# One 128x128 stationary shape for all attention products: zero-padded keys, values in pairs of heads, the forgetting decay in the padded rows

## The reference

```python
# forgetting attention: a decay is added to the logits of each head
log_f = log_sigmoid(f_logit + b_f)
cum = cumsum(log_f, axis=1)                       # (B, H_FOX, S)
logits = einsum('bhqd,bhkd->bhqk', q, k) * scale + cum[..., :, None] - cum[..., None, :]
out = einsum('bhqk,bhkd->bhqd', masked_softmax(logits, causal), v)

# dilated windows, differential attention, selected keys: the same two products
qk = rms_norm(q, gain_q), rms_norm(k, gain_k)
logits = einsum('bqhe,bkhe->bhqk', *qk) * 64 ** -0.5 + bias     # masked with -inf
out = einsum('bhqk,bkhe->bqhe', softmax(logits), v)
```

## Time and profile before

| | |
|---|---|
| median of three runs | 2591.96 us (2590.84 to 2592.58) |
| span of the profiled execution | 2591.7 us |
| TensorE busy in it | 2371.6 us |
| VectorE busy | 1063.7 us |
| ScalarE busy | 963.4 us |
| GpSimd busy | 388.2 us |
| TensorE's mean granted clock | 0.955 |

### The profile page before, as it was taken

One profiled execution on the slowest core, in us unless ns is written; L12 is line 12 of the kernel. 1 busy time (PEld: TensorE's weight loads), 2 busy tenths in 40 slices (PEclk: granted clock), 3 DMA queues, 4 the chain that ended last, 5 costly groups with the idle time before them and its releaser, 6 DMA issues. The chain is left out here.

```text
span 2591.7 us, 30357 instructions
## 1 busy us (share of the span) xinstructions
PE 2371.6 (92%) x11019; PEld 1828.8 (71%) x11019; DVE 1063.7 (41%) x1957; ACT 963.4 (37%) x1410; POOL 388.2 (15%) x375
## 2 busy tenths in 40 slices
PE   6699887999799989899999999984899998999999
PEld 3479684567388868578878787951557886788787
DVE  6484444343554432332223333148464334333322
ACT  2133213343455532344432212348456433444311
POOL 0010321131122210111110000124241000122200
PEclk7798998999899999899999999997999999999999
DMA  6871001101133333123333233200011323233331
GB/s 231 287 211 41 1 1 46 57 1 33 57 90 96 97 94 100 33 81 97 97 93 101 75 88 97 82 13 17 13 54 52 95 80 98 82 96 97 94 101 64
DMA packets 348925, 210.42 MB, mean 81 GB/s; under 512 B 21293, under 2 KB 329699, under 8 KB 348798
## 3 DMA queue, kind: packets, MB, share of 16 engines
q1 hardware_dynamic: 347691, 208.37, 27.0%
q10 hardware_dynamic: 1139, 0.82, 0.1%
HBM read 206.48 MB, written 9.24 MB: 83 GB/s over the span
## 5 line engine op out<-in xcount | busy, mean ns | idle before, releaser
L236 PE MATMUL ffn_up_psum<-h_hi,ffn_up_w_hi 128*128 128x512 f32 x704 | 275.3, 391 | 0.0
L237 PE MATMUL ffn_up_psum<-h_lo,ffn_up_w_hi 128*128 128x512 f32 x704 | 274.1, 389 | 0.0
L238 PE MATMUL ffn_up_psum<-h_hi,ffn_up_w_lo 128*128 128x512 f32 x704 | 274.1, 389 | 0.0
L331 DVE TENSOR_TENSOR ffn_up_w_lo<-ffn_up_raw,ffn_up_w_hi 128x1024 fp32r<-128x1024 f32 x88 | 107.7, 1225 | 326.5 <-ACT ffn_up_w_hi L327 326.5
L327 ACT ACTIVATE ffn_up_w_hi<-ffn_up_raw 128x1024 fp32r<-128x1024 f32 x88 | 93.1, 1060 | 165.6 <-PE ffn_up_psum L238 162.4
L236 PEld LDWEIGHTS ffn_up_psum<-h_hi,ffn_up_w_hi 128*128 128x128 f32 x704 | 132.6, 188 | 28.8 <-DVE ffn_up_w_lo L331 1.3
L237 PEld LDWEIGHTS ffn_up_psum<-h_lo,ffn_up_w_hi 128*128 128x128 f32 x704 | 132.3, 188 | 28.2 <-issue 0.6
L238 PEld LDWEIGHTS ffn_up_psum<-h_hi,ffn_up_w_lo 128*128 128x128 f32 x704 | 132.3, 188 | 27.1
L236 PE MATMUL ffn_down_psum<-ffn_hidden_hi,ffn_down_w_hi 128*128 128x512 f32 x352 | 138.2, 392 | 0.0
L236 PE MATMUL conv_up_psum<-h_hi,conv_up_w_hi 128*128 128x512 f32 x352 | 137.6, 391 | 0.0
L237 PE MATMUL conv_up_psum<-h_lo,conv_up_w_hi 128*128 128x512 f32 x352 | 137.4, 390 | 0.0
(11 more groups left out here) (650 smaller groups left out, 5414.8 us busy)
## 6 DMA issues: line engine op xcount, KB each, us to landing
conv_up_raw<-in_ffn_up_dram SPq DMA_DIRECT2D x44, 512.0 KB, 3.7
ffn_up_raw<-in_ffn_w_gate_dram SPq DMA_DIRECT2D x44, 512.0 KB, 3.7
ffn_up_raw<-in_ffn_w_up_dram SPq DMA_DIRECT2D x44, 512.0 KB, 3.7
ffn_down_raw<-in_ffn_w_down_dram SPq DMA_DIRECT2D x32, 704.0 KB, 4.5
in_a_mod_slots<-in_ada_w_dram SPq DMA_DIRECT2D x16, 1024.0 KB, 6.8
branches_raw<-in_w_in_dram SPq DMA_DIRECT2D x24, 512.0 KB, 3.6
down_raw<-in_ffn_down_dram SPq DMA_DIRECT2D x16, 704.0 KB, 4.6
mod_slots<-in_ada_w_dram SPq DMA_DIRECT2D x4, 2048.0 KB, 13.9
```

Of the source, the lines that this page charges most:

```text
L236: pe.matmul(out, w_hi, r_hi, start=start, stop=False)
L237: pe.matmul(out, w_hi, r_lo, start=False, stop=False)
L238: return pe.matmul(out, w_lo, r_hi, start=False, stop=stop)
L331: dve.tensor_tensor(self.lo[:, j % PAIRS], self.raw[:, j], self.hi[:, j % PAIRS].bitcast(F32), ALU.subtract)\
```

## The change

Every stationary operand of the attention becomes 128x128.

- **Keys.** The keys of an even head keep the lower 64 partitions of their tile, and the upper 64 become zero; the keys of an odd head move to the upper half of a tile of their own, with zeros below. A score streams the whole tile over all 128 rows against a stationary tile that holds both heads' queries. `fox` and the two uncompressed branches of `nsa` get their odd tiles (queries too in `fox`) from the new class HalfTiles, which GpSimd runs at the head of its queue in `rwkv_chunks`. The tiles of the second block are split in `select_and_norm`: GpSimd writes zeros into the odd tiles first, then for each of eleven key tiles does two half products and a memset in place of one product. The compressed keys get a second tile by two half copies and a memset in `nsa_compress`.
- **Values.** A weighing takes the values of two heads (128 columns); the half of the result that belongs to the other head isn't read. So an output group is one head in place of two, and each of `finish_act` and `finish_dve` runs twice as often, over 64 partitions (`keep_halves`).
- **Decay.** In `fox` the 64 rows of a head's tile that belong to no channel of it hold the decay: row 0 of the rest of the queries' tile is `cum` against -1 in row 0 of the keys' rest, and row 32 of the keys' rest is `cum` against 1 in the queries' rest; all other rows of the keys' rest are zero. (The scores of this kernel are negated logits: VectorE takes their minimum and ScalarE the exponential of their negative.) `cum` gets there by one-row DMAs. Twelve such DMAs are issued by SyncE in `nsa_compress`, and waited for there. The extra product, `left`, `right`, `gates`, `heads` and `prepare` go.
- **Places.** `w_idx` moves into the unused columns of `vc`, the penalty is packed without its unused part, and the buffers `squares` and `scaled` move into `o` and `o_b`.

```diff
@@ CoarsePiece.score
-                mm = pe.matmul(psum[:, first:first + n], self.nq[rows, p, i * P:(i + 1) * P], self.kcmp[rows, 0:n],
+                mm = pe.matmul(psum[:, first:first + n], self.nq[:, p, i * P:(i + 1) * P], self.kcmp[:, self.a, 0:n],
@@ rwkv_chunks, GpSimd's queue
+            halves.by_pool(pool, halves_copied)
             for i in range(7 * NCH):
@@ attention
-            if prepare is not None:
-                n_prepared = prepare(pool, prepared)
...
-                    out = psum[unit.rows, bank(unit.group), unit.tile * P:(unit.tile + 1) * P]
+                    out = psum[:, bank(unit.group), unit.tile * P:(unit.tile + 1) * P]
@@ fox_decay
-        c.add(dve.memset(left[:], 1.0))
-        c.add(dve.memset(right[:], 1.0))
...
-        c.link(dve.tensor_tensor_scan(left[0:H_FOX], ones[:], n[:], 0.0, ALU.mult, ALU.add))
-        c.add(dve.tensor_copy(left[HD:HD + H_FOX], left[0:H_FOX]))
-        for base in (32, HD + 32):
-            c.add(dve.tensor_scalar(right[base:base + H_FOX], left[0:H_FOX], -1.0, None, ALU.mult))
+        c.link(dve.tensor_tensor_scan(e[:], ones[:], n[:], 0.0, ALU.mult, ALU.add))
...
+    @block.sync
+    def _(sp):
+        sp.wait_ge(v, 6)
+        for h in range(H_FOX):
+            rest = (1 - h % 2) * HD
+            for dst, row in ((fox_q[h], rest + CUM_ROW), (fox_k[h], rest + ONE_ROW)):
+                sp.dma_start(dst[row:row + 1], e[h:h + 1]).then_inc(placed, 16)
+        sp.wait_ge(placed, 16 * 2 * H_FOX)
@@ HalfTiles (new)
+    def by_pool(self, pool, copied):
+        tiles = self.fox_q + self.fox_k + self.keys
+        lower, upper = slice(0, HD), slice(HD, P)
+        for _, odd in tiles:
+            fill = 1.0 if any(odd is q for _, q in self.fox_q) else 0.0
+            pool.memset(odd[lower], fill)
+        for even, odd in tiles:
+            pool.tensor_copy(odd[upper], even[upper]).then_inc(copied, 1)
+        pool.wait_ge(copied, len(tiles))
+        for even, odd in tiles:
+            fill = 1.0 if any(odd is q for _, q in self.fox_q) else 0.0
+            pool.memset(even[upper], fill).then_inc(copied, 1)
+        pool.wait_ge(copied, 2 * len(tiles))
+        for even, odd in self.fox_k:
+            pool.memset(even[HD + CUM_ROW:HD + CUM_ROW + 1], -1.0).then_inc(copied, 1)
+            pool.memset(odd[CUM_ROW:CUM_ROW + 1], -1.0).then_inc(copied, 1)
+        pool.wait_ge(copied, 2 * len(tiles) + 2 * len(self.fox_k))
@@ fox_attention
-                units.append(Unit([Piece(q[:, tokens], k, lambda j, h=h: fv[:, j, h * HD:(h + 1) * HD], 0, (i + 1) * P,
-                                         table[:, (TT - 1 - i) * P:], extra=(left[rows, tokens], gates[rows, p]))],
-                                  p, rows, i))
+                units.append(Unit([Piece(fox_q[h][:, i * P:(i + 1) * P], fox_k[h], lambda j, pair=pair: fv[:, j, pair], 0,
+                                         (i + 1) * P, table[:, (TT - 1 - i) * P:])], h, i))
@@ keep_halves (new)
+    def high(act, h, o):
+        return act.activation(out[h // 2][0][rows(h % 2)], o[rows(source(h))], ACT.Copy)
+
+    def low(dve, h, o):
+        hi, lo = (x[rows(h % 2)] for x in out[h // 2])
+        return dve.tensor_tensor(lo, o[rows(source(h))], hi.bitcast(F32), ALU.subtract)
@@ nsa_compress, VectorE
-            dve.tensor_copy(kcmp[:], psum[:, 4, 0:N_CMP])
+            for a_ in range(2):
+                half = slice(a_ * HD, (a_ + 1) * HD)
+                dve.tensor_copy(kcmp[half, a_], psum[half, 4, 0:N_CMP])
@@ select_and_norm, GpSimd
+            for zero in zeros:
+                c.add(pool.memset(zero, 0.0))
             for g, members in enumerate(groups):
                 pool.wait_ge(rooted, g + 1)
                 for n in members:
                     pool.wait_ge(scaled, n + 1)
-                    pool.tensor_tensor(heads[n], heads[n], rstd[:, g % 2, n % group], ALU.mult).then_inc(normed, 1)
+                    factor = rstd[:, g % 2, n % group]
+                    if odd_keys[n] is None:
+                        c.settle()
+                        pool.tensor_tensor(heads[n], heads[n], factor, ALU.mult).then_inc(normed, 1)
+                        continue
+                    pool.wait_ge(normed, n)
+                    c.settle()
+                    c.add(pool.tensor_tensor(odd_keys[n][upper], heads[n][upper], factor[upper], ALU.mult))
+                    pool.tensor_tensor(heads[n][lower], heads[n][lower], factor[lower], ALU.mult).then_inc(normed, 1)
+                    c.settle()
+                    c.add(pool.memset(heads[n][upper], 0.0))
```

More of the change, by code:

```diff
@@ L1313, in by_tensor, with rwkv_chunks @@
         mm.then_inc(self.bonus_summed, 1)
-def rwkv_chunks(nc, old, square, r_in, a_in, k_in, b_in, v_in, tot, mid, y):
+def rwkv_chunks(nc, old, square, r_in, a_in, k_in, b_in, v_in, tot, mid, y, halves):
     H = 4
@@ new lines, in fox_attention, with keep_halves, rows @@
+        attention(nc, old, "fox", units, [(table[:], tables_dram[TAB_FOX])], *keep_halves(out, lambda h: h % 2),
+                  tables_out=tables_out)
+def keep_halves(out, source):
+    def rows(half):
+        return slice(half * HD, (half + 1) * HD)
+    def high(act, h, o):
[3 more added lines that the diff above has]
+        return dve.tensor_tensor(lo, o[rows(source(h))], hi.bitcast(F32), ALU.subtract)
+    return high, low
@@ L2214, in _ @@
             dve.memset(vcmp[:], 0.0)
+            dve.memset(kcmp[:], 0.0)
             gains_of(dve)
@@ L2239, in _, with nsa_attention @@
             last.then_inc(kept, 1)
-def nsa_attention(nc, old, nq, nk, nv, kcmp, vcmp, gates, tables_dram, out, beside, load_next):
+def nsa_attention(nc, old, nq, keys, nv, kcmp, vcmp, gates, tables_dram, out, beside, load_next):
     with ExitStack() as ctx:
@@ L2465, in view, with first_block @@
     return w.rearrange("(k p) n -> p k n", p=P)
-def first_block(nc, old, A, x_t, store_scale, tables_out, late, gains, mod, cols, square, scratch, heads, b_f, ends, x_rstd, begin,
+def first_block(nc, old, A, x_t, store_scale, tables_out, late, gains, mod, cols, square, scratch, b_f, ends, x_rstd, begin,
                 spread):
@@ L2576, in first_block @@
                     load_out1 = next(out1)
-                    nsa_attention(nc, old, nq, nk, nv, kcmp, vcmp, gates, scratch, [tile(y_pair, 5 + c) for c in range(3)],
+                    nsa_attention(nc, old, nq, halves.keys, nv, kcmp, vcmp, gates, scratch, [tile(y_pair, 5 + c) for c in range(3)],
                                   SplitBeside([y_r[:, k] for k in range(2)], [0, 0], [tile(y_pair, k) for k in range(2)]),
@@ L2642, in dilated_attention, with keep @@
                           for g in range(1, A_GROUPS)]
-            attention(nc, old, "dil", units, loads,
-                      lambda act, g, o: act.activation((wide if g % 2 else near)[:, g // 2], o, ACT.Copy),
+            def keep(act, g, o):
+                rows = slice(g % 2 * HD, (g % 2 + 1) * HD)
+                return act.activation((wide if g % 4 >= 2 else near)[rows, g // 4], o[rows], ACT.Copy)
+            attention(nc, old, "dil", units, loads, keep,
                       stats=(least, sums), cover_fill=True)
@@ L3254, in build @@
         gains = sb("gains", [P, 4 * KD])
-        heads = sb("heads", [P, H_FOX // 2])
         b_f = sb("b_f", [H_FOX, 1])
```

163 lines of the change are left out of this document (78 added, 85 removed).

## The result

The changed kernel takes 2565.39 us (median of four runs, 2564.63 to 2565.75), the kernel before beside it 2591.4 (2590.44 to 2592.58): a ratio of 0.9884, interval 0.9858 to 0.9911. It is faster by 26 us, half of the 51 that were forecast, and 4 us over the range's upper end of 2561.

A forecast was written before the change was run, and what follows sets the result against it. TensorE alone was taken to set the pace in the attention stages. From the span of 2591.7 us, -73.5 (attention) + 14.5 (`rwkv_chunks`) + 8 (`select_and_norm`) + 0.2 (`nsa_compress`) gave 2541 us; range about 2520 to 2561.

The forecast's parts named there:

- The loss at a change of shape: Attention on TensorE: a round loses 0.485 us wherever the stationary operand's shape changes three times; one shape removes it.
- Rival 3: Attention: the loss at a group's start is the semaphore wait, not the shape; only the decay's 12.9 goes; 2602 us, chance 0.03.
- rival 4: Attention on TensorE: weight loads are not hidden in one shape, 80 us would show; 2621 us, chance 0.01.
- What is late next: Attention: other engines fill up as output groups double, VectorE in `fox` at 10.0 against TensorE's 10.9; four stages give 73.5 us.
- the sum of 82.5: Gain in us over `fox` 23.1, `nsa` 25.9, `dil` 15.9 and `last` 17.6, before allowing for other engines.
- rival 1: Attention: the other engines cap it, so it gives 56 us in place of 73.5; 2558 us, chance 0.15.
- GpSimd in `rwkv_chunks`: Half tiles at the head of GpSimd's queue take 19.3 us before the first `quarter`; the stage ends 14.5 us later.
- The price of a memset: GpSimd's memset of 64x512 was taken as 0.5 us, nearer the copy's 0.66 than the 0.10 of 128x1.
- rival 2: GpSimd's memset is cheap (0.1), with delays of 3.3 and 5; 2527 us, chance 0.14.
- `select_and_norm`: Each split key tile costs GpSimd 1.9 us more; the last five make the stage end 8 us later.
- `nsa_compress`: The split copy of the compressed keys adds 0.2 us.
- the twelve DMAs: One-row DMAs on SP in `nsa_compress`, 0.34 us each to issue, hidden behind VectorE's copies with some 3 us to spare.

The follow-up runs named there:

- `e7_values`: Changed kernel with all weights at their old distance and one head's values alone as stationary operand again (128x64), scores still 128x128: 2571.9 us in one run.
- `e8_rows`: Changed kernel, weights at their old distance, values in pairs, but scores of `nsa` (not coarse), `dil` and `last` over their head's 64 rows again: 2582.54 us, one run.
- `e1_room`: Changed kernel with an unused tensor where `heads` lay, moving later left-side tensors up by 32 bytes: 2541.55 us, ratio 0.9789 to the kernel before.
- `e2_before_moved`: Kernel before with `heads` put on the right side of SBUF, so later left-side tensors move down by 32 bytes, same instructions: 2623.21 us, ratio 1.0126.
- `e3_offsets`: Kernel before with the weights of eight single stages moved up by 32 to 192 unused bytes, their moving operands staying: 2620.19 us in one run.
- `e4_sides`: Kernel before with 32 unused bytes displacing only low weights in `conv_up`, only high weights in `ffn2_up`, the moving operand in `branches`: 2607.86 us in one run.

## Why the prediction was wrong, point by point

**The loss at a change of shape** was right in mechanism and size. It was read from two stretches with the same kinds of groups (the earlier trace rows against the earlier trace rows), which differ in the stage too; `e7_values` and `e8_rows`, which differ from the changed kernel in the shape alone, gave it back stage by stage to within 1 us, but for `nsa` in `e8_rows` (15.8 for 18), where the three that were added for its fillers look like too many. (In reading the prediction has the other engines busy for a third to 70%; GpSimd is at 23 to 49%. Nothing hangs on it.) Rival 3 (the wait) and rival 4 (loads not hidden in one shape) are out. With it falls, for this kernel, the rule of the Trainium skill that the prediction set against it (TensorE: Matmul & The Clock Gate, Part 3): weighings in one shape follow each other at 0.11 us, each with a load of its own.

**What is late next** was the term of the attention that was mis-sized: 9 us were taken off the sum of 82.5 for covers that would run out, and all but 0.7 of them came; the prediction's other figure, 81 if all covers hold, was the right one. In `fox` the step that failed is the count of VectorE's time. The prediction took the 1.15 us in which it waits for ScalarE as work, and so came to 10.0 of 10.9. The rows of after, VectorE at the end of a head, TensorE beside it, and a window of eight scores that holds two such subtractions (columns as in the earlier trace rows):

```profile
469.49 0.69 DVE L2141 TENSOR_TENSOR y_lo<-fox_psum,y_hi 64x512 fp32r<-64x512 f32 x1 [1.10 <-ACT y_hi L2137]
468.68 1.02 PE L1753 MATMUL fox_psum<-mix_pj 128*128 128x512 f32 x2
469.54 0.27 PE L1933 MATMUL fox_psum<-square,fox_scores 128*128 128x128 f32 x1
463.80:474.79 10.99, 10.99 (x77) 9.09 (x76) 7.29 (x38) 7.61 (x23) 4.23 (x9) 1.00 0.00 0
```

The wait is still there, but the score that VectorE would turn to next starts on TensorE at 468.68, and the group behind it at 469.54: there was nothing else to do. VectorE is busy for 7.29 of 10.99 us with both subtractions (the 6.63 further above hold one), and rival 1, drawn up on the same count, is out.

**GpSimd in `rwkv_chunks`**: +14.2 against +14.5, a hit that is luck in part, as two errors nearly cancel. The memsets of one row are six and not twelve (two for each of three pairs), so that the work took 16.7 us (275.26 to 291.96) in place of 19.3; and GpSimd enters the stage 1.7 us behind TensorE, which the sum left out. The price of a memset, 0.5 by the nearest row, was right (0.48 to 0.60), and rival 2 (0.1) is out. The Trainium skill (GPSIMD Engine Reference, Instruction dispatch) has each core of GpSimd go on by itself; in these rows memsets of the lower and copies of the upper half follow each other without gain, 0.57 to 0.60 each.

**`select_and_norm`** (+8.2 against +8) and **`nsa_compress`** (+0.3 against +0.2) were right; the twelve DMAs took longer to issue than reckoned, 435.44 to 442.98 in SP's queue in place of 4 us, and were hidden all the same, as VectorE copied until 445.48.

**What failed** is a step that wasn't there. The prediction costs the removal of `left`, `right`, `gates` and `heads` by the work they took part in, and the part "Places" of the change not at all. That a tensor's removal or growth moves every later one, and that the moved ones are operands of some 4700 products in other stages, was missed: 30.3 us, more than the whole of GpSimd's added work that it weighed at length. Of these, 24.6 fall to the stages that `heads` alone displaced, and 5.7 to `in_2a` to `in_2c`, which `w_idx` and `vc` displaced too. Without it the time would be, by estimate, 2565.4 - 30.3 = 2535, inside the range and 6 us under the forecast; by the spans, on which the sum was made, 8 under it, which are the attention's. `e1_room` and `e2_before_moved` show this cause from both sides, `e3_offsets` and `e4_sides` what of the move matters. None of the rivals had a place for it: all of them asked how the edited stages would go.

## What to carry to other kernels

When a change adds, drops or resizes a buffer, compare the addresses of all operands that the dense stages stream, not only those of the edited ones: here the removal of a constant of 12 bytes and the move of `w_idx` into a larger `vc` took back more than a third of the attention's gain. Read matmul pace from start to start in every stage after a change; a stage that is slower from its first product to its last, at the same granted clock, is a reason to look at its operands' places. And work that is put on an idle engine is free only behind that engine's last step on the path: the same 16.7 us of GpSimd cost 14 to 15 at the head of its queue and nothing at its end.

## What the runs showed of the hardware that was not expected

- An fp32r product of 512 columns starts 227 ns after the last where weights and moving operand are a multiple of 256 bytes apart in a partition, and 229 to 234 ns on average of the three at the other distances tried (32 to 224 in steps of 32). The Trainium skill (TensorE: Matmul & The Clock Gate, Part 2, Step-by-step) says that loading the next weights takes no SBUF bandwidth from the running matmul, as the two have ports of their own; the runs here differ by 1 to 3%, so the measurement decides: the pace is not independent of where both lie. What lies under this wasn't found.
- GpSimd's time goes by the elements of a partition, not by their rows: a memset of one row of 512 takes 0.52 us as one of 64 rows does, and half a product (64x512) 1.26 as a whole one (1.24). So splitting a tile by partitions into two products doubles its cost there.
